# The last expert's down matrix, multiplied by column halves, and the final norm behind it

## The chip, the cores and the metric

One core of one Trainium2 chip runs the whole kernel. The metric is the device time of one launch in microseconds (us), as the median of several executions. Beside it stands one profiled execution, whose trace gives every instruction's start and duration. TensorE is called PE, VectorE DVE, ScalarE ACT, GpSimd POOL and SyncE SP, as in the profile.

## The reference, cut to what matters

A decoder block on 256 tokens of width 1024: a Mamba-2 mixer and a sparse attention mixer, merged, and then a mixture of experts over 32 experts with the top 4 per token, all in float32. The change is in the end of the expert stage and in the final norm:

```python
out = jnp.zeros_like(t)
for e in range(N_EXPERTS):
    a = clamped_swiglu(t @ w_gate_up[e] + b_gate_up[e])
    out = out + combine[:, e:e + 1] * (a @ w_down[e] + b_down[e])
...
x = x + out
return rms_norm(x, final_norm_w)      # x / sqrt(mean(x*x) + eps) * w
```

## The kernel before, in words

**Experts.** Each expert gets up to 64 of its tokens (CAP = 64). A gate/up matrix has 8 MB and a down matrix 4 MB; SP streams them through four places in SBUF of 4 MB each. PE counts finished pieces in `unit_done`, and SP waits for that count before it loads over a place. A hardware loop does most experts; the last ones are written out with finer pieces. Experts go in pairs (s = 0, 1); the last expert has s = 1.

**A down product.** With 64 tokens the stationary operand is 128 rows by 64 columns, so two matmuls can sit side by side on the two halves of TensorE's columns; `128*64` in a row of the profile says that. Before the change the two halves hold the two column halves of the result: tokens by columns 0 to 511 on partitions 0 to 63, tokens by columns 512 to 1023 on partitions 64 to 127, both in one PSUM bank. The contraction has 1024 rows, in 8 steps r of 128; partition p of the place holds rows 8p to 8p+7 of the matrix, so step r is a column range of the place. `ATL` holds the last expert's activations, transposed.

**The last down matrix.** SP loads it in five transfers by steps (`LAST_ROWS`: steps 0-1, 2-3, 4-5, 6, 7; L663 to L669). The first two wait for unit 11, the other three for unit 12, which are the two halves of the down product that used the place before. PE (L1442 to L1452) takes the steps in order, waiting for each transfer, and after step 1 runs `combine` for the expert before.

**Combine.** ACT copies the PSUM bank to SBUF (`down_out`, L1717), and `combine` (L1343 to L1353) multiplies it by the matrix of routing weights (`CTS`, 64 slots by 128 tokens) into four banks, for two token halves t and two column halves h. As h = 1 lies on partitions 64 to 127, the four matmuls have 64 rows each (`64*128`), and two sit on the two row halves of the array. `CTS` holds the weights twice, on both halves of the partitions.

**The end.** DVE adds each of the four results to X (`final_added`, L2316). ACT squares and sums each (L1768). Then each token half has its own mean, root and reciprocal. DVE multiplies token half 0 by reciprocal and norm weight (L2331, two instructions); POOL has meanwhile multiplied token half 1 by the norm weight (L834) into `XW`, which DVE and ACT scale (L2349, L1775). SP stores token half 0 in one transfer (L671), token half 1 in two (L674). A table of ACT's functions is loaded at L1764, before the squares.

Of the kernel before, what the change touches and what calls it, by code (L numbers as in the profile page):

```python
# [29 lines left out]
ALU = mybir.AluOpType  # L30
ACT = mybir.ActivationFunctionType
AX = mybir.AxisListType

P = 128
# [31 lines left out]
LAST_ROWS = ((0, 2), (2, 4), (4, 6), (6, 7), (7, 8))  # L66
# [125 lines left out]
def hybrid_block(nc, x, mix_norm_w, w_in, conv_w, conv_b, dt_bias, a_log, d_skip, ssm_norm_w,  # L192
# [3 lines left out]
    with ExitStack() as ctx:  # L196
# [149 lines left out]
        YSL2 = part(ZS, 512, 512)  # L346
# [23 lines left out]
        XW = part(ring, T * D, D)  # L370
# [9 lines left out]
        last_full = [sem(f"last_full{i}") for i in range(len(LAST_ROWS))]  # L380
# [122 lines left out]
        def _(sp):  # L503
# [161 lines left out]
            for (r0, r1), full in zip(LAST_ROWS, last_full):  # L665
                if r0 % 4 == 0:
                    sp.wait_ge(unit_done, units_to(last * 2, 11 + r0 // 4))
                sp.dma_start(places[LOOP_SLOT[9]][:, D * r0:D * r1], down_rows(EXPERTS - 1)[:, D * r0:D * r1]
                             ).then_inc(full, 16)  # L669
            sp.wait_ge(norm_ready, 2)  # L670
            sp.dma_start(out[0, 0:P], RJ[:, 0]).then_inc(stored, 16)  # L671
            for h, (normed, n) in enumerate(((norm_ready, 3), (norm_in, 1))):
                sp.wait_ge(normed, n)
                sp.dma_start(out[0, P:2 * P, 512 * h:512 * h + 512], RJ[:, 1, 512 * h:512 * h + 512]).then_inc(stored, 16)  # L674
            sp.wait_ge(stored, 16 * (T + 1))
# [3 lines left out]
        def _(pool):  # L679
# [150 lines left out]
            pool.wait_ge(wfn_ready, 2)  # L830
            for h in range(2):
                pool.wait_ge(final_in, 3 + h)
                cols = slice(512 * h, 512 * h + 512)
                g.tensor_tensor(XW[:, cols], X[:, 1, cols], WFN[:, cols], ALU.mult).then_inc(xw_ready, 1)  # L834


        @block.tensor
        def _(pe):
# [504 lines left out]
            def combine(n, s, y=YSB, first=True, final=True, halves=False):  # L1343

                pe.wait_ge(y_ready, n + 1)
                if first:
                    pe.wait_ge(o_read, n * 2 + 1)
                for t in range(T):
                    for h in range(2):
                        r = slice(64 * h, 64 * h + 64)  # L1350
                        ins = mm(psum[:, 3 + 2 * t + h, :], CTS[r, s, t], y[r, :], start=first, stop=final)  # L1351
                        if final and (h or halves):
                            ins.then_inc(o_full, 1)  # L1353
# [89 lines left out]
            for (r0, r1), full in zip(LAST_ROWS, last_full):  # L1443
                pe.wait_ge(full, 16)
                w = places[LOOP_SLOT[9]]
                for r in range(r0, r1):
                    for h in range(2):
                        ins = mm(psum[64 * h:64 * h + 64, 0, :], ATL[:, r % 4, 64 * (r // 4):64 * (r // 4) + 64],
                                 w[:, D * r + 512 * h:D * r + 512 * h + 512], start=(r == 0), stop=(r == 7))
                if r1 % 4 == 0:  # L1450
                    ins.then_inc(unit_done, 1)
                if r1 == 2:  # L1452
                    combine(last * 4 + 3, 0, final=False)
            combine(last * 4 + 4, 1, YSL2, first=False, halves=True)


        @block.scalar
        def _(act):
# [303 lines left out]
            down_out(units_to(last * 2 + 1, 8), 0, YSL2)  # L1762

            a(junk[:, 0:1], ss[:, 6:7], ACT.Sqrt)  # L1764
            for t in range(T):
                for h in range(2):
                    act.wait_ge(final_in, 2 * t + h + 1)
                    a(SQX[:, t, 512 * h:512 * h + 512], X[:, t, 512 * h:512 * h + 512], ACT.Square,  # L1768
# [606 lines left out]
```

## Time and profile before

| | us |
|---|---|
| median of 3 executions | 1250.89 |
| lowest and highest | 1250.57, 1251.33 |
| the profiled execution | 1252.41 |
| its span, first to last instruction | 1250.7 |
| PE busy in the span | 1187.8 |
| DVE, ACT, POOL busy | 438.1, 288.5, 112.6 |

The profiled execution takes 1.7 us beside its span. Times in the rows below count from the start of the span. A matmul in float32 shows as two records in the trace: `x8` in a row of L1448 or L1351 is four matmuls. The busy times are sums over the whole span and say nothing of which engine the last microseconds wait for.

### The profile page before, as it was taken

The numbers are of one execution on the slowest core, as the hardware profiler recorded it, in microseconds if no ns is written. First come the engines' busy times: TensorE is split into PE (matmuls) and PEld (weight loads), VectorE is DVE, ScalarE is ACT, GpSimd is POOL, SyncE is SP. The second block draws the span as 40 slices with busy tenths as digits, with TensorE's granted clock in tenths as the row PEclk, the third lists the DMA queues.
The fourth block names the chain that finished last, engine by engine and source line by source line (L and its number), as shares of the span: only waits on it lengthen the run. The fifth ranks groups of instructions, "written<-read, shape, count | busy, mean of one in ns | idle before, by whom it ended". The sixth has DMA issues, their size and how long they took to land.

```text
span 1250.7 us, 16280 instructions
## 1 busy us (share of the span) xinstructions
PE 1187.8 (95%) x6644; PEld 622.4 (50%) x6644; DVE 438.1 (35%) x868; ACT 288.5 (23%) x522; POOL 112.6 (9%) x99
## 2 busy tenths in 40 slices
PE   8999999999999999999999989898999989898996
PEld 8999988788743434434343424242333324242432
DVE  7876567767331221312122221212221212122112
ACT  6574457653410101101010100010110101010112
POOL 2202213345400000000000000000000000000000
PEclk9999999999999999999999999999999999999999
DMA  8747534239999999999999999999999999999995
GB/s 272 209 146 231 164 107 135 102 104 393 402 397 418 428 430 431 431 432 430 433 431 434 430 433 431 434 431 432 431 434 432 431 431 434 432 431 431 425 426 220
DMA packets 60988, 453.57 MB, mean 363 GB/s; under 512 B 9096, under 2 KB 33808, under 8 KB 45328
## 3 DMA queue, kind: packets, MB, share of 16 engines
q1 hardware_dynamic: 60640, 452.75, 88.1%
q8 instruction: 32, 0.52, 0.2%
q10 hardware_dynamic: 304, 0.20, 0.1%
q14 instruction: 12, 0.10, 0.0%
HBM read 451.88 MB, written 1.05 MB: 362 GB/s over the span
## 4 chain that ended last, share of the span: by engine, by line
PE 63%; DMA 28%; ACT 3%; DVE 3%; issue 1%; POOL 0%; SPq 0%; DVEq 0%; ACTq 0%
PE psum L1313 23%; DMA ring<-in_w_gate_up_dram 14%; DMA slot<-in_w_gate_up_dram 12%; PE psum L1325 11%; PE psum L940 9%; PE psum L1281 5%; PE psum L906 4%; PE psum L1351 3%; PE psum L842 3%; DMA ring<-in_w_down_dram 3%; PE psum L943 2%; ACT WH L1484 1%; ACT XDT L1663 1%; PE psum L1191 1%; DVE XDT L2144 1%
## 5 line engine op out<-in xcount | busy, mean ns | idle before, releaser
L1313 PE MATMUL psum<-ring,ZS 128*64 128x512 f32 x1512 | 345.9, 601 | 13.9 <-DMA ring<-in_w_gate_up_dram 13.5
L1313 PEld LDWEIGHTS psum<-ring,ZS 128*64 128x64 f32 x1512 | 105.8, 137 | 216.9 <-issue 196.8
L2290 DVE TENSOR_TENSOR X<-X,psum 128x1024 f32<-128x1024 f32 x62 | 72.9, 1218 | 373.7 <-PE psum L1351 373.6
L1325 PE MATMUL psum<-ring,HT 128*64 128x512 f32 x736 | 168.2, 610 | 22.7 <-DMA ring<-in_w_down_dram 22.7
L1313 PE MATMUL psum<-slot,ZS 128*64 128x512 f32 x512 | 119.8, 612 | 10.2 <-DMA slot<-in_w_gate_up_dram 10.2
L2272 DVE TENSOR_SCALAR ZS<-psum 128x512 f32<-128x512 f32 x32 | 22.1, 692 | 298.9 <-PE psum L1313 298.9
L1325 PEld LDWEIGHTS psum<-ring,HT 128*64 128x64 f32 x736 | 57.5, 140 | 126.1 <-issue 125.1
L1804 DVE TENSOR_TENSOR WL<-ring,WH 128x2048 fp32r<-128x2048 f32 (+1 forms) x42 | 96.1, 2287 | 38.6 <-ACT WH L1484 38.2
L1713 ACT ACTIVATE HT<-psum 128x512 f32<-128x512 f32 x31 | 18.5, 597 | 313.8 <-PE psum L842 313.8
L834 POOL TENSOR_TENSOR ring<-X,YV 128x512 f32<-128x512 f32 x2 | 2.9, 1489 | 909.9 <-DVE X L2316 909.9
L1484 ACT ACTIVATE WH<-ring 128x2048 fp32r<-128x2048 f32 (+1 forms) x42 | 78.8, 1877 | 10.7 <-PE psum L906 6.8
L1313 PEld LDWEIGHTS psum<-slot,ZS 128*64 128x64 f32 x512 | 35.3, 139 | 78.9 <-issue 61.1
L1717 ACT ACTIVATE HT<-psum 128x512 f32<-128x512 f32 x31 | 18.5, 597 | 209.8 <-PE psum L1325 209.8
L1351 PE MATMUL psum<-HT,QT 64*128 64x512 f32 x256 | 63.6, 615 | 0.0
L1281 PEld LDWEIGHTS psum<-QT,XC 128*128 128x128 f32 x480 | 54.7, 192 | 12.2 <-issue 12.2
L1281 PE MATMUL psum<-QT,XC 128*128 128x128 f32 x480 | 57.6, 278 | 0.0
L1325 PE MATMUL psum<-slot,HT 128*64 128x512 f32 x256 | 56.7, 595 | 0.0
L1709 ACT ACTIVATE ZS<-ZS 128x512 f32<-128x512 f32 x32 | 20.1, 629 | 114.5 <-DVE ZS L2272 114.5
L940 PE MATMUL psum<-HTH,WH 128*128 128x256 f32 x304 | 44.1, 288 | 0.0
L940 PE MATMUL psum<-HTL,WH 128*128 128x256 f32 x304 | 42.7, 283 | 0.0
L940 PE MATMUL psum<-HTH,WL 128*128 128x256 f32 x304 | 42.6, 283 | 0.0
L1351 PEld LDWEIGHTS psum<-HT,QT 64*128 64x128 f32 x256 | 22.0, 186 | 41.0 <-issue 41.0
(383 smaller groups left out, 1254.5 us busy)
## 6 DMA issues: line engine op xcount, KB each, us to landing
ring<-in_w_gate_up_dram SPq DMA_DIRECT2D x38, 4096.0 KB, 29.1
ring<-in_w_down_dram SPq DMA_DIRECT2D x18, 4096.0 KB, 30.7
slot<-in_w_gate_up_dram SPq DMA_DIRECT2D x12, 4096.0 KB, 28.6
ring<-in_w_gate_up_dram SPq DMA_DIRECT2D x18, 2048.0 KB, 13.2
ring<-in_w_in_dram SPq DMA_DIRECT2D x29, 1024.0 KB, 7.0
slot<-in_w_down_dram SPq DMA_DIRECT2D x7, 4096.0 KB, 30.8
ring<-in_w_down_dram SPq DMA_DIRECT2D x9, 2048.0 KB, 16.1
slot<-in_w_gate_up_dram SPq DMA_DIRECT2D x8, 2048.0 KB, 15.2
```

What stands on the lines that cost most here:

```text
L842: return nc.tensor.transpose(o, i, IDN[:, :])
L906: ins = mm(bank(b, 512), src[:, 4 * h + k, P * t:P * t + P], w[:, k, :], start=(h == 0 and n == 0 and k == 0), stop=(h == 1 and n == 2 and ...
L940: ins = mm(bank(b, 2, SEQ)[:, half], w[:, k, rows], src[:, k, :], start=(n == 0 and k == 0), stop=(n == 2 and k == KT - 1))
L943: ins = mm(bank(b, 2, nco)[:, half], src[:, k, rows], w[:, k, :], start=(n == 0 and k == 0), stop=(n == 2 and k == KT - 1))
L1281: ins = mm(bank(5 + k // 4, P, off=P * (k % 4)), H2[:, t, P * k:P * k + P], SPR[:, t].rearrange("p a b -> p (a b)"), start=(t == 0), stop= ...
L1313: ins = mm(psum[64 * (c % 2):64 * (c % 2) + 64, c // 2, :], XTS[:, k, s], every_other_run(row, c), start=False, stop=(k == KT - 1))
L1325: ins = mm(psum[64 * h:64 * h + 64, 2, :], lhs, w[:, at:at + 512], start=(k == 0), stop=(k == 7))
L1351: ins = mm(psum[:, 3 + 2 * t + h, :], CTS[r, s, t], y[r, :], start=first, stop=final)
L1484: a(WH[i % SPLITS][:, 0:n], slot_view(u, n), ACT.Copy).then_inc(wh_ready, 1)
L1804: v.tensor_tensor(WL[i % SPLITS][:, 0:n], slot_view(u, n), WHF[i % SPLITS][:, 0:n], ALU.subtract).then_inc(wl_ready, 1)
L2272: v.tensor_scalar(GBU.rearrange("p (q f) -> p q f", q=2), gu[:, :, :, 0], 7.0, None, ALU.min).then_inc(g_ready, 1)
L2290: v.tensor_tensor(xo, xo, psum[:, 3 + 2 * t:5 + 2 * t, :], ALU.add).then_inc(o_read, 1)
```

## The change: what it does

The last down matrix comes in six transfers. Step k now means the rows 4a+k of each partition for both contraction halves a = 0, 1: `k=0` and `k=1` whole (1 MB each), then k = 2 and 3 in columns 0 to 511 (512 KB each, one semaphore), then k = 2 and k = 3 in columns 512 to 1023 (512 KB each). All of them follow one wait, for unit 12. On PE the two halves of TensorE's columns hold the two contraction halves, and the column halves of the result lie in two banks. So partitions 0 to 63 and 64 to 127 of a bank are two partial sums of the same 64 tokens, and the matmul with `CTS` that follows has all 128 rows, which adds them. `combine` for the expert before moves behind the column half 0. ACT copies the two banks separately. In the norm, both token halves of columns 0 to 511 are weighted on DVE and scaled on ACT, those of columns 512 to 1023 are done on DVE, POOL does nothing, and the output leaves in two transfers by column halves. DVE squares and sums one of the four quarters.

The diff, without the renamed constants and tiles (`YL` is two tiles in place of `YSL2`, and `XW` has both token halves):

```diff
-            for (r0, r1), full in zip(LAST_ROWS, last_full):
-                if r0 % 4 == 0:
-                    sp.wait_ge(unit_done, units_to(last * 2, 11 + r0 // 4))
-                sp.dma_start(places[LOOP_SLOT[9]][:, D * r0:D * r1], down_rows(EXPERTS - 1)[:, D * r0:D * r1]
-                             ).then_inc(full, 16)
-            sp.wait_ge(norm_ready, 2)
-            sp.dma_start(out[0, 0:P], RJ[:, 0]).then_inc(stored, 16)
-            for h, (normed, n) in enumerate(((norm_ready, 3), (norm_in, 1))):
-                ...
+            last_place = places[LOOP_SLOT[9]].rearrange("p (a k n) -> p a k n", a=2, k=4)
+            last_rows = w_down[0, EXPERTS - 1].rearrange("(p a k) n -> p a k n", a=2, k=4)
+            def last_part(k, c0, c1, full):
+                sp.dma_start(last_place[:, :, k, c0:c1], last_rows[:, :, k, c0:c1]).then_inc(full, 16)
+            sp.wait_ge(unit_done, units_to(last * 2, 12))
+            last_part(0, 0, D, last_full[0])
+            last_part(1, 0, D, last_full[1])
+            last_part(2, 0, 512, last_full[2])
+            last_part(3, 0, 512, last_full[2])
+            last_part(2, 512, D, last_full[3])
+            last_part(3, 512, D, last_full[4])
+            outs = out[0].rearrange("(t p) n -> p t n", p=P)
+            for h, normed in ((0, norm_in), (1, norm_ready)):
+                cols = slice(512 * h, 512 * h + 512)
+                sp.wait_ge(normed, T)
+                sp.dma_start(outs[:, :, cols], RJ[:, :, cols]).then_inc(stored, 16)
...
-            pool.wait_ge(wfn_ready, 2)
-            for h in range(2):
-                pool.wait_ge(final_in, 3 + h)
-                cols = slice(512 * h, 512 * h + 512)
-                g.tensor_tensor(XW[:, cols], X[:, 1, cols], WFN[:, cols], ALU.mult).then_inc(xw_ready, 1)
...
+            def last_pair(k, h):
+                for a in range(2):
+                    at = 4096 * a + 1024 * k + 512 * h
+                    ins = mm(psum[64 * a:64 * a + 64, h, :], ATL[:, k, 64 * a:64 * a + 64], w[:, at:at + 512],
+                             start=(k == 0), stop=(k == 3))
+                if k == 3:
+                    ins.then_inc(unit_done, 1)
+            def last_combine(t, h):
+                mm(psum[:, 3 + 2 * t + h, :], CTS[:, 1, t], YL[h], start=False, stop=True).then_inc(o_full, 1)
+            for k in range(2):
+                pe.wait_ge(last_full[k], 16)
+                last_pair(k, 0)
+                last_pair(k, 1)
+            pe.wait_ge(last_full[2], 16 * 2)
+            last_pair(2, 0)
+            last_pair(3, 0)
+            combine(last * 4 + 3, 0, final=False)
+            pe.wait_ge(y_ready, last * 4 + 5)
+            last_combine(0, 0)
+            for k in range(2, 4):
+                pe.wait_ge(last_full[1 + k], 16)
+                last_pair(k, 1)
+            last_combine(1, 0)
+            pe.wait_ge(y_ready, last * 4 + 6)
+            last_combine(0, 1)
+            last_combine(1, 1)
...
             down_out(units_to(last * 2 + 1, 6))
-            down_out(units_to(last * 2 + 1, 8), 0, YSL2)
+            down_out(units_to(last * 2 + 1, 7), 0, YL[0])
             a(junk[:, 0:1], ss[:, 6:7], ACT.Sqrt)
+            down_out(units_to(last * 2 + 1, 8), 1, YL[1])
+            for n, (t, h) in enumerate(((0, 0), (1, 0), (0, 1))):
+                act.wait_ge(final_in, n + 1)
+                a(SQX[:, t, cols], X[:, t, cols], ACT.Square, accum_out=RT[:, 9, t, h:h + 1]).then_inc(ss_ready, 1)
+            act.wait_ge(ss_ready, 5)
             for t in range(T):
-                ...
+                act.wait_ge(lg_ready, 2 + t)
                 a(ss[:, 2 + t:3 + t], RT[:, 9, t, 1:2], ACT.Sqrt, scale=1.0 / D, bias=ss[:, t:t + 1]).then_inc(sq_root, 1)
+            act.wait_ge(lg_ready, 4)
+            for t in range(T):
+                act.wait_ge(xw_ready, t + 1)
+                a(RJ[:, t, 0:512], XW[:, t], ACT.Copy, scale=ss[:, 4 + t:5 + t]).then_inc(norm_in, 1)
...
+            final_added(0, 0, 0)
+            first_weighted(0)            # XW[:, t] = X[:, t, 0:512] * WFN[:, 0:512]
+            final_added(1, 1, 0)
+            final_added(2, 0, 1)
+            final_added(3, 1, 1)
+            dve.wait_ge(ss_ready, 4)
+            v.tensor_scalar(ss[:, 0:2], RT[:, 9, :, 0], 1.0 / D, EPS, ALU.mult, ALU.add).then_inc(lg_ready, 1)
+            dve.wait_ge(final_in, 4)
+            v.tensor_tensor_reduce(SQX[:, 1, 512:D], X[:, 1, 512:D], X[:, 1, 512:D], 1.0, 0.0, ALU.mult, ALU.add,
+                                   RT[:, 9, 1, 1:2]).then_inc(lg_ready, 1)
+            first_weighted(1)
+            dve.wait_ge(sq_root, 5)
+            v.reciprocal(ss[:, 4:6], ss[:, 2:4]).then_inc(lg_ready, 1)
+            dve.wait_ge(lg_ready, 4)
+            for t in range(T):
+                v.scalar_tensor_tensor(out=RJ[:, t, 512:D], in0=X[:, t, 512:D], scalar=ss[:, 4 + t:5 + t],
+                                       in1=WFN[:, 512:D], op0=ALU.mult, op1=ALU.mult).then_inc(norm_ready, 1)
```

## Rows read from the trace of the kernel before

**Rows 1.** The page's part 4: share of the span in the chain that ended last.

```profile
PE 63%; DMA 28%; ACT 3%; DVE 3%; issue 1%; POOL 0%; SPq 0%; DVEq 0%; ACTq 0%
```

**Rows 2.** The chain, its last transfer: start us, us, what.

```profile
1190.21 31.76 DMA ring<-in_w_down_dram
```

**Rows 3.** The issue of the five last loads (timeline: start us, us, engine, line).

```profile
1199.05 13.74 SPq L668 DMA_DIRECT2D ring<-in_w_down_dram  x5
```

**Rows 4.** Loads issued at 1199.05, 1199.4, 1202.5, 1202.9, 1205.4: KB, us to landing.

```profile
ring<-in_w_down_dram SPq DMA_DIRECT2D x1, 1024.0 KB, 30.4
...
ring<-in_w_down_dram SPq DMA_DIRECT2D x1, 1024.0 KB, 32.5
...
ring<-in_w_down_dram SPq DMA_DIRECT2D x1, 1024.0 KB, 31.9
...
ring<-in_w_down_dram SPq DMA_DIRECT2D x1, 512.0 KB, 32.7
...
ring<-in_w_down_dram SPq DMA_DIRECT2D x1, 512.0 KB, 31.5
```

**Rows 5.** PE, ACT's copy and table load from 1222 us on, in the timeline.

```profile
1222.11 3.65 PE L1325 MATMUL psum<-ring,HT 128*64 128x512 f32 x16 [1.33 <-DMA ring<-in_w_down_dram]
...
1229.76 1.89 PE L1448 MATMUL psum<-ring,ZS 128*64 128x512 f32 x8
...
1231.58 1.99 PE L1351 MATMUL psum<-HT,QT 64*128 64x512 f32 x8
...
1233.50 5.37 PE L1448 MATMUL psum<-ring,ZS 128*64 128x512 f32 x24
...
1238.91 0.60 ACT L1717 ACTIVATE ZS<-psum 128x512 f32<-128x512 f32 x1 [8.34 <-PE psum L1448]
1239.53 1.28 ACT L1764 ACT_TABLE_LOAD   x1
...
1239.57 1.99 PE L1351 MATMUL psum<-ZS,QT 64*128 64x512 f32 x8 [0.70 <-ACT ZS L1717]
```

**Rows 6.** ACT's two copies behind the 16 whole-array matmuls of L1281, in one loop pass.

```profile
1050.96 0.60 ACT L1704 ACTIVATE ZS<-psum 128x512 f32<-128x512 f32 x1 [0.62 <-PE psum L1281]
...
1052.74 0.60 ACT L1704 ACTIVATE ZS<-psum 128x512 f32<-128x512 f32 x1 [1.19 <-PE psum L1281]
```

**Rows 7.** Windows: us, busy PE, PEld, DVE, ACT, POOL, then PEclk, DMA share, GB/s.

```profile
280.00:290.00 10.00, 9.68 (x54) 7.61 (x54) 5.69 (x7) 2.74 (x4) 8.27 (x9) 1.00 1.08 320
1100.00:1150.00 50.00, 45.08 (x226) 17.72 (x223) 8.46 (x10) 4.84 (x8) 0.00 (x0) 1.00 1.00 432
1248.00:1249.00 1.00, 0.00 (x0) 0.00 (x0) 0.00 (x0) 0.00 (x0) 0.00 (x0) 0.50 0.97 379
```

**Rows 8.** The final norm in the timeline, DVE, ACT, POOL and the first store.

```profile
1240.72 1.88 DVE L2316 TENSOR_TENSOR X<-X,psum 128x512 f32<-128x512 f32 x3 [16.72 <-PE psum L1351]
...
1242.59 0.68 DVE L2316 TENSOR_TENSOR X<-X,psum 128x512 f32<-128x512 f32 x1
...
1242.75 2.94 POOL L834 TENSOR_TENSOR ring<-X,YV 128x512 f32<-128x512 f32 x2 [909.89 <-DVE X L2316]
...
1243.41 1.16 DVE L2331 SCALAR_TENSOR_TENSOR ring<-X,ss,YV 128x512 f32<-128x512 f32 x1
...
1244.56 1.68 DVE L2331 SCALAR_TENSOR_TENSOR ring<-X,ss,YV 128x512 f32<-128x512 f32 x1
...
1246.16 0.15 DVE L2326 RECIPROCAL ss<-ss 128x1 f32<-128x1 f32 x1
1246.27 0.35 SPq L671 DMA_DIRECT2D out_dram<-ring  x1
1246.41 0.72 ACT L1775 ACTIVATE ring<-ring,ss 128x512 f32<-128x512 f32 x1 [1.38 <-DVE ss L2326]
```

**Rows 9.** DVE by line and form: busy us, mean ns.

```profile
L1787 DVE CUSTOM_DVE_ANT_0 YV<-X 128x1024 f32<-128x1024 f32 x1 | 1.2, 1226 | 2.1 <-DMA X<-in_x_dram 2.1
...
L2144 DVE CUSTOM_DVE_ANT_0 XDT<-psum,CM 128x256 f32<-128x256 f32 x20 | 7.2, 418 | 0.0
```

More of the change, by code:

```diff
@@ L65 @@
 LAST_WHOLE = 3
-LAST_ROWS = ((0, 2), (2, 4), (4, 6), (6, 7), (7, 8))
+LAST_PARTS = 5
 OFF_Z, OFF_XBC, OFF_DT, OFF_Q = 0, 1024, 3072, 3088
@@ L345, in hybrid_block @@
         ATL = part(ZS, 0, 4, P)
-        YSL2 = part(ZS, 512, 512)
+        YL = [part(ZS, 512, 512), part(ZS, 1024, 512)]
         SGA = part(ZS, 1024, 512)
@@ L369, in hybrid_block @@
         RJ = part(ring, 0, T, D)
-        XW = part(ring, T * D, D)
+        XW = part(ring, T * D, T, 512)
         RCI = sb("RCI", [P, 1], I32)
@@ L379, in hybrid_block @@
         unit_done = sem("unit_done")
-        last_full = [sem(f"last_full{i}") for i in range(len(LAST_ROWS))]
+        last_full = [sem(f"last_full{i}") for i in range(LAST_PARTS)]
         x_in = [sem(f"x_in{t}") for t in range(T)]
@@ L1341, in weights_turned, with combine @@
                 ins.then_inc(ct_full, 1)
-            def combine(n, s, y=YSB, first=True, final=True, halves=False):
+            def combine(n, s, final=True):
                 pe.wait_ge(y_ready, n + 1)
-                if first:
-                    pe.wait_ge(o_read, n * 2 + 1)
+                pe.wait_ge(o_read, n * 2 + 1)
                 for t in range(T):
@@ L1350, in combine @@
                         r = slice(64 * h, 64 * h + 64)
-                        ins = mm(psum[:, 3 + 2 * t + h, :], CTS[r, s, t], y[r, :], start=first, stop=final)
-                        if final and (h or halves):
-                            ins.then_inc(o_full, 1)
+                        ins = mm(psum[:, 3 + 2 * t + h, :], CTS[r, s, t], YSB[r, :], start=True, stop=final)
+                    if final:
+                        ins.then_inc(o_full, 1)
             pe.wait_ge(h2n_ready, T)
@@ L1442, in _ @@
             pe.wait_ge(at_ready, last * 4 + 4)
[L1443 to L1450, printed above, removed]
-                    ins.then_inc(unit_done, 1)
-                if r1 == 2:
-                    combine(last * 4 + 3, 0, final=False)
-            combine(last * 4 + 4, 1, YSL2, first=False, halves=True)
+            w = places[LOOP_SLOT[9]]
+            def last_pair(k, h):
[4 more added lines that the diff above has]
+                if k == 3:
+                    ins.then_inc(unit_done, 1)
+            def last_combine(t, h):
[17 more added lines that the diff above has]
+            last_combine(1, 1)
         @block.scalar
@@ L2311, in _, with final_added @@
             gated(last * 4 + 4, units_to(last * 2 + 1, 4), last * (2 * per) + (per + base + 1))
-            def final_added(t, h):
-                dve.wait_ge(o_full, last * 8 + (2 * t + h + 7))
+            def final_added(n, t, h):
+                dve.wait_ge(o_full, last * 8 + (7 + n))
                 xo = X[:, t, 512 * h:512 * h + 512]
                 v.tensor_tensor(xo, xo, psum[:, 3 + 2 * t + h, :], ALU.add).then_inc(final_in, 1)
-            def first_half_mean(t):
-                dve.wait_ge(ss_ready, 3 + 2 * t)
-                v.tensor_scalar(ss[:, t:t + 1], RT[:, 9, t, 0:1], 1.0 / D, EPS, ALU.mult, ALU.add).then_inc(lg_ready, 1)
@@ L2336, in _, with first_weighted @@
[L2336 to L2349 removed]
+            def first_weighted(t):
+                dve.wait_ge(final_in, 1 + t)
+                v.tensor_tensor(XW[:, t], X[:, t, 0:512], WFN[:, 0:512], ALU.mult).then_inc(xw_ready, 1)
```

36 lines of the change are left out of this document (2 added, 34 removed).

## The prediction

> **What bounds the kernel now.** I read the chain of waits first. Of the whole span it runs 63% through PE and 28% through loads [rows 1]: the expert stage streams at 432 GB/s with the DMA engines at a share of 1.00 and PE busy 45.1 of 50 us [rows 7], so both are near full. Nothing of the change touches that stage, so only the last 50 us count. There the chain's last transfer, 31.76 us from 1190.21 [rows 2], is the first half of the down matrix before the last; PE starts on it at 1222.11 [rows 5], and from there PE works without a wait for data to its last down step. The reader is to see in the timeline [rows 5] that PE begins the last matrix at 1229.76 and runs 2 steps, a combine and 6 steps back to back. Step length: 6 steps in the row from 1233.50, less its pipeline tail, or 4 matmuls (x8) from 1229.76 to about 1231.48; 0.86 us per step.
>
> Then I set the landings [rows 3, 4] beside it: issue time plus flight gives 1229.5, 1231.9, 1234.4, 1235.6 and 1236.9 for steps 0-1, 2-3, 4-5, 6 and 7. PE asks for them at 1229.76, 1233.50, 1235.2, 1236.9 and 1237.8. So the loads lead PE by only 0.3 to 1.6 us, and the combine put after step 1 is what keeps PE busy while steps 2-3 arrive. The end is PE-bound with the loads close behind.
>
> After the last step (ends about 1238.7) come ACT's copy at 1238.91, the last combine at 1239.57, the first add of DVE at 1240.72, the last add's end at 1243.27, and the first store's issue at 1246.27 [rows 5, 8]. The span ends at 1250.7, 4.43 after that issue. In between the three stores, 1.05 MB, flow at 379 GB/s [rows 7], that is about 2.8 us without a pause: the end hangs on the first store's issue, not on the last one.
>
> **The change, part by part.** All durations are of the profiled execution (1252.41, of which 1.7 lie outside the span); a difference found in its span is added to the median, 1250.89.
>
> *Loads.* The wait for unit 12 delays the first two issues by 3.4 us (1199.05 to 1202.5). Their data flew 30 us behind a full queue, and what was issued before them lands until about 1227.1 (1229.5 less the 2.4 that 1 MB takes), so this costs nothing; it would cost only if the queue ran dry, which is 25 us away. SP now posts six transfers, with two pieces per partition in each. Before, the last five took 13.74 us to post as SP waited for room [rows 3]. It will now be later in posting, which is free as long as the queue keeps work; behind SP's posting wait only the stores, 30 us later. Pieces are 4 KB for k = 0, 1 and 2 KB for the column halves. The two 512 KB loads with 4 KB pieces landed 1.2 and 1.3 us after the load before, and the 1 MB ones with 8 KB pieces 2.4 and 2.5: no difference; I add 0.1 for k = 1. For 2 KB pieces the trace shows no load at a full queue. Bounds: the rate of the stage, 432 GB/s (no cost), and 320 GB/s of the stretch 280 to 290, with smaller pieces among them [rows 7]. Nearest are the stores, whose second half has 2 KB pieces: 379 at a share of 0.97, or 391 when full, 10% slower. Taken: 2.7 us per MB. Landings: k=0 1229.5, k=1 1232.0, column half 0 (k=2, 3) 1234.7, the rest 1236.1 and 1237.4.
>
> *PE.* k = 0: 1229.76 to 1231.48. The combine that filled the gap is gone from here, so PE waits until 1232.0 + 0.15 and works to 1233.87. It waits again for column half 0, to 1234.85, and works two pairs to 1236.57. Two waits, 0.67 and 0.98, that did not exist. Then combine of the expert before, 1.72. Then the first last_combine. This is a new form, 128 rows by 128 columns by 512, one at a time. Its price: L1281's matmuls are whole-array ones of 128 columns, and ACT's copies behind each eight start 1.78 us apart [rows 6], 0.2225 each, four times that at most for 512 columns, 0.89; the lower bound is that of a 64-row pair, 0.43 for each. The 64-row pairs gave four matmuls in 1.72 because two ran at once, so a single one is 0.86, as is a single one of L1281 without its overhead. Taken: 0.86. So the last combine costs 4 x 0.86 = 3.44 in place of 1.72, and partial sums added inside the array are paid with PE time. Its first quarter comes before the last columns, three quarters behind them.
>
> At each change between the forms, PE starts later than the matmul count says: 0.10 from 1231.48 to 1231.58, 0.20 from 1233.30 to 1233.50 [rows 5]. There are four changes now instead of the two before the final wait; I charge 0.10, 0.20, 0.15, 0.15. This is where a rule of the Trainium skill bears: "TensorEngine Tiling (Array Packing)", section "Key Properties", says that a change of tiling mode, not of tile, drains the engine. It gives no price. By the rule every one of the four costs something and the sum keeps its 0.6; without it the sum would be 0.6 smaller. The gaps speak for the rule.
>
> In order: combine 1236.67 to 1238.39, last_combine(0,0) 1238.59 to 1239.45, the pairs of k = 2, 3 in column half 1 (their data there since 1237.4) 1239.6 to 1241.3, then from 1241.45 three last_combines to 1244.0. ACT's copy of column half 0 (1236.6 to 1237.3) hides behind combine; the table load of 1.28 hides behind PE's work to 1241.3; the copy of half 1 takes 0.60 plus 0.2 of latency and hides behind last_combine(1,0). That hiding is the gain of the change: the 0.9 us between 1238.66 and 1239.57 go. Sum on PE: waits +1.65, combines +1.72, form changes +0.3, k=0 to the end otherwise equal, hidden copy -0.9: +2.8, and by the times above the last matmul ends at 1244.0 and not at 1241.3 (1239.57 + 1.72), +2.7.
>
> *Adds.* Before, DVE's four adds queued behind each other from 1240.72 to 1243.27; the last came 2.0 after PE's end. Now three are early, and the last starts 0.29 after PE's end (as 1240.72 stands to 1239.57 + 0.86) and ends at 1245.0: +1.7 here, so 1.0 comes back.
>
> *Norm.* On DVE behind the last add: the small mean 0.15; square-and-sum of one quarter, interpolated between 418 ns for 256 columns and 1226 for 1024 [rows 9] 0.69, plus 0.08 to read the sum; first_weighted(1) about 0.65; reciprocal 0.15: to 1246.7. ACT's roots hide behind first_weighted(1). ACT then scales two quarters, 0.72 each at most: 1248.15, and the first store is issued. DVE's two weighted products take 1.16 each, or 1.68 each where POOL ran beside it [rows 8]; POOL is idle now, so 1249.0 is taken (up to 1250.1). Before, the step from the last add's end to the first store was 3.0, now 3.15. POOL's 2.94 go, and were off the path except for the 0.5 by which a product beside it was longer.
>
> *Stores.* 1 MB in 2 KB pieces: 4.43 from first issue to the end as before, as the flow of 2.8 is the same within 0.1. The second store is issued at 1249.0, 0.85 later, while 1.4 us of the first flow: no gap. Even at 1250.1 its 1.4 us of flow and a base of 1.4 end at about 1252.9, 0.4 before the end's own tail, a loss of up to 0.7. End of the span: 1248.15 + 4.43 = 1252.6, +1.9. Forecast: 1250.89 + 1.9 = 1252.8 (a profiled execution of 1254.3).
>
> **The rivals.** About 0.2%, 2.5 us, is what can be told from no change; the forecast lies 0.6 short of that.
>
> *The waits go away (1251.1 to 1251.3).* If k = 1 and column half 0 were there when PE asks (1231.5 and 1233.2), 1.65 would go: +0.25. It would need the last loads to land 1.5 us earlier. For it: the five flights took between 30.4 and 32.7 us [rows 4], so a landing can move by 2. Against: nothing in the change makes the queue before these loads shorter, and the pieces get smaller. Chance 0.17.
>
> *Column-cut loads are slow (1255.0), the case on the slower side.* Mechanism: the flow at 320 GB/s [rows 7] instead of 431 from k = 0 on. k = 1 lands at 1233.7, column half 0 at 1236.9, the last at 1240.2. From 1233.87 on, each microsecond by which column half 0 is late moves the end by one: PE starts it at 1237.05 instead of 1234.85, +2.2, in all +4.1. The last load then still leads PE (1241.8). At full price it needs 4 KB pieces slow too, against which the 512 KB loads' 1.2 and 1.3 us speak. Chance 0.13. The Trainium skill's "DMA: Bandwidth & Descriptors", section "Bandwidth", asks for transfers of at least 1 MiB and gives 341 GB/s for one of 1 MB alone; by it the column halves would take 3.1 us per MB and the end come 0.4 later than forecast. The landings of the 512 KB loads at over 400 GB/s show no such price in a full queue.
>
> *Posting stalls.* SP posts 12 pieces per partition where it posted 5, and must find room for them [rows 3]. If the last transfer is posted so late that it lands after 1240.5, when PE needs it, the excess is added: up to 3, so 1253 to 1256. Against: posting keeps pace with draining, as in the stage. Chance 0.06.
>
> *PE's clock falls in the new waits.* It fell to 0.50 only in the idle stretch at the end [rows 7] and the stage with a wait of 1.33 before 1222.11 [rows 5] ran its steps at the same 0.86 before and after. At 1.2 GHz in place of 2.4 the remaining 9 us of work would double: about 1260. Chance 0.02.
>
> *Faster by more than 2.5 us.* Both waits gone (-1.65), whole-array matmuls at 0.43 each (-1.3 on the path) and a norm chain 1.5 shorter would all be needed, to under 1248.4. Chance 0.03.
>
> **How the numbers follow.** The forecast has 0.59, with an own range of 1251.6 to 1254.2 (form changes and new matmul -0.8 to +0.2, landings -0.3 to +0.7, norm and stores -0.3 to +0.7); about a third of it lies above 1253.4, 0.18. Slower by over 0.2%: 0.18 + 0.13 + 0.04 + 0.02 = 0.37. Faster by over 0.2%: 0.03. Within: 0.60. The range for 8 in 10 takes in the case of the waits gone and that of slow loads nearly whole: 1251.0 to 1255.2.
>
> **What would show it.** In the timeline after: L1448's successor with a gap of 0.6 to 0.7 before k = 1 and one near 1.0 before column half 0, both put down to the loads; four whole-array matmuls (`128*128 128x512`) of 0.86 each; no wait for ACT before the last two; DVE's adds with idle time between them; the first store at about 1248.2. Wrong would be: no waits of PE for data behind 1229.76; a whole-array matmul at under 0.6; last load landing after 1240; the first store before 1247.5 or after 1249; a different time at 1229.76, which would mean that the stage before has moved.

## The result

The changed kernel takes 1253.47 us (median of 12 runs, 1252.79 to 1255.43) against 1251.22 for the kernel before (12 runs, 1250.42 to 1252.92). The ratio is 1.0017, with a 95% interval of 1.0010 to 1.0025: slower by about 2.1 us, inside the 0.2% that counted as no change (the interval reaches past it), and clearly above zero. The profiled execution took 1253.09, its span 1251.3.

The profile after, the last matrix and the norm. First PE in the timeline (start us, us, engine, line, operation, tiles, shape), as [rows 5] for before:

```profile
1228.67 1.89 PE L1452 MATMUL psum<-ring,ZS 128*64 128x512 f32 x8
...
1231.02 1.94 PE L1452 MATMUL psum<-ring,ZS 128*64 128x512 f32 x8 [0.46 <-DMA ring<-in_w_down_dram]
...
1233.65 1.94 PE L1452 MATMUL psum<-ring,ZS 128*64 128x512 f32 x8 [0.70 <-DMA ring<-in_w_down_dram]
...
1235.52 1.99 PE L1354 MATMUL psum<-HT,QT 64*128 64x512 f32 x8
...
1237.44 1.12 PE L1459 MATMUL psum<-ZS,QT 128*128 128x512 f32 x2
...
1238.49 1.94 PE L1452 MATMUL psum<-ring,ZS 128*64 128x512 f32 x8
...
1240.36 2.84 PE L1459 MATMUL psum<-ZS,QT 128*128 128x512 f32 x6
```

The reader is to see the two new waits for loads in brackets, and that from 1235.52 on PE has no gap: nobody waits for ACT's copies any more. The last line is three whole-array matmuls; DVE's adds behind them, here in the timeline, start 0.86 apart because each has to wait for one of them, where before they followed each other at 0.62 [rows 8]:

```profile
1241.52 0.69 DVE L2342 TENSOR_TENSOR X<-X,psum 128x512 f32<-128x512 f32 x1 [1.51 <-PE psum L1459]
...
1242.38 0.69 DVE L2342 TENSOR_TENSOR X<-X,psum 128x512 f32<-128x512 f32 x1 [0.17 <-PE psum L1459]
...
1243.24 0.69 DVE L2342 TENSOR_TENSOR X<-X,psum 128x512 f32<-128x512 f32 x1 [0.17 <-PE psum L1459]
...
1243.96 0.69 DVE L2358 CUSTOM_DVE_ANT_0 XC<-X 128x512 f32<-128x512 f32 x1
...
1244.58 0.69 DVE L2347 TENSOR_TENSOR ring<-X,YV 128x512 f32<-128x512 f32 x1
...
1245.37 1.33 ACT L1800 ACTIVATE ring<-ring,ss 128x512 f32<-128x512 f32 x2 [0.38 <-DVE ss L2362]
1245.37 1.42 DVE L2365 SCALAR_TENSOR_TENSOR ring<-X,ss,YV 128x512 f32<-128x512 f32 x2
1246.73 0.93 SPq L683 DMA_DIRECT2D out_dram<-ring  x2
```

The loads issued at 1202.91, 1203.6, 1210.45 (k = 3, column half 0), 1218.4 and 1222.9, one row of the transfers for each, KB and us to landing. (The load of k = 2, column half 0, shares its semaphore with k = 3, so its own landing can't be read.)

```profile
ring<-in_w_down_dram SPq DMA_DIRECT2D x1, 1024.0 KB, 25.5
...
ring<-in_w_down_dram SPq DMA_DIRECT2D x1, 1024.0 KB, 27.4
...
ring<-in_w_down_dram SPq DMA_DIRECT2D x1, 512.0 KB, 23.2
...
ring<-in_w_down_dram SPq DMA_DIRECT2D x1, 512.0 KB, 16.5
...
ring<-in_w_down_dram SPq DMA_DIRECT2D x1, 512.0 KB, 13.3
```

They land at 1228.4, 1231.0, 1233.6, 1234.9 and 1236.2. Their flights are shorter than those of [rows 4], but that doesn't mean faster loads here, the loads were issued later into the same queue.

**How to compare two profiles here.** PE begins the last matrix at 1229.76 before and at 1228.67 after. That 1.1 arises before the last matrix, in matmuls that the change leaves as they are; in the other ten profiles PE begins it between 1227.67 and 1230.18. So all profiles are compared from the first matmul of the last matrix to the end of the span: 20.94 before, 22.63 after, +1.69. Column "from" in this table gives that stretch less 20.94; "ratio" is from the timed runs, each against runs of the kernel before on the same chip (us worked out with 1251.2). The first column has two limits. Spans are read to 0.1, so it is good to about 0.1. And where the first load is late, PE's wait for it lies ahead of the stretch and isn't counted: 0.46 in e4 and 0.65 in e6 by the brackets.

| kernel | from, us | ratio (95% interval) | us |
|---|---|---|---|
| changed | +1.69 | 1.0017 (1.0010 to 1.0025) | +2.1 |
| e1 combine first | +1.05 | 1.0007 (0.9997 to 1.0016) | +0.9 |
| e2 new norm alone | +0.88 | 1.0008 (0.9999 to 1.0017) | +1.0 |
| e3 norm on DVE | -1.35 | 0.9989 (0.9980 to 0.9998) | -1.4 |
| e4 half rows | +1.55 | 1.0013 (1.0004 to 1.0023) | +1.6 |
| e5 POOL beside | +2.79 | 1.0023 (1.0014 to 1.0032) | +2.9 |
| e6 one wait | -0.01 | 0.9998 (0.9989 to 1.0007) | -0.3 |
| e7 whole steps | +3.25 | 1.0031 (1.0019 to 1.0043) | +3.9 |
| e8 row halves side by side | +1.30 | 1.0008 (0.9999 to 1.0017) | +1.0 |
| e9 tokens first | -0.07 | 0.9998 (0.9989 to 1.0007) | -0.3 |
| e10 combine late | +1.49 | 1.0006 (0.9997 to 1.0015) | +0.8 |

The two columns agree within 0.7 everywhere. An interval is about 1 us to either side, so steps under 1 us are read from the profiles, one execution each, and the timed runs only say that nothing contradicts them.

### The profile page after: what moved, and what is told of

It reads as the page before. It is cut to its first block, busy times and chain, and to the rows that moved or that the text cites. A ratio compares the mean times of both kernels' runs of the same rounds, so it can differ in the third digit from the quotient of the medians.

```text
span 1251.3 us, 16275 instructions
## 1 busy us (share of the span) xinstructions
PE 1191.3 (95%) x6644; PEld 623.9 (50%) x6644; DVE 438.2 (35%) x869; ACT 289.0 (23%) x522; POOL 110.2 (9%) x97
## 3 DMA queue, kind: packets, MB, share of 16 engines
HBM read 451.88 MB, written 1.05 MB: 362 GB/s over the span
## 4 chain that ended last, share of the span: by engine, by line
PE 63%; DMA 28%; ACT 3%; DVE 3%; issue 1%; SPq 1%; POOL 0%; DVEq 0%; ACTq 0%
PE psum L1317 23%; DMA ring<-in_w_gate_up_dram 14%; DMA slot<-in_w_gate_up_dram 12%; PE psum L1329 11%; PE psum L944 9%; PE psum L1285 5%; PE psum L910 4%; PE psum L1354 3%; PE psum L846 3%; PE psum L947 2%; DMA ring<-in_w_down_dram 2%; ACT WH L1507 1%; ACT XDT L1686 1%; PE psum L1195 1%; SPq L670 1%
## 5 line engine op out<-in xcount | busy, mean ns | idle before, releaser
L1329 PE MATMUL psum<-ring,HT 128*64 128x512 f32 x736 | 171.6, 620 | 21.5 <-DMA ring<-in_w_down_dram 21.5
L1317 PE MATMUL psum<-slot,ZS 128*64 128x512 f32 x512 | 116.4, 597 | 7.7 <-DMA slot<-in_w_gate_up_dram 7.7
L944 PEld LDWEIGHTS psum<-HTH,WH 128*128 128x128 f32 x304 | 39.1, 191 | 0.8 <-issue 0.6
```

The lines of the kernel that those rows point to most:

```text
L944: ins = mm(bank(b, 2, SEQ)[:, half], w[:, k, rows], src[:, k, :], start=(n == 0 and k == 0), stop=(n == 2 and k == KT - 1))
L1317: ins = mm(psum[64 * (c % 2):64 * (c % 2) + 64, c // 2, :], XTS[:, k, s], every_other_run(row, c), start=False, stop=(k == KT - 1))
L1329: ins = mm(psum[64 * h:64 * h + 64, 2, :], lhs, w[:, at:at + 512], start=(k == 0), stop=(k == 7))
```

## The experiments

**e1: the combine back where it covers a load.**

```diff
             for k in range(2):
                 pe.wait_ge(last_full[k], 16)
                 last_pair(k, 0)
                 last_pair(k, 1)
+                if k == 0:
+                    combine(last * 4 + 3, 0, final=False)
...
-            combine(last * 4 + 3, 0, final=False)
```

> The changed kernel with one move: the combine of the expert before stands right after k = 0 again, not behind column half 0. Theory (PE bounds the end, and two waits for loads that the old combine used to fill are part of the loss): PE's waits before k = 1 and column half 0, 0.46 and 0.70 us in the profile of the changed kernel, go, and the time falls by 1.0 to 1.3 us, to 0.7 to 1.2 above the kernel before. Behind column half 0 there is then no 64-row combine left to cover ACT's copy, so up to 0.2 may come back as a wait for ACT. Rival 1 (late loads set the end): the last pairs wait for their loads instead, and the time stays within 0.3 of the changed kernel's. Rival 2 (norm and stores are the loss): no difference either, since only slack is moved.

The timed runs gave back 1.2, the profile 0.64. The waits for loads are gone, and the cover for ACT's copy with them, in the timeline of e1:

```profile
1232.59 3.65 PE L1452 MATMUL psum<-ring,ZS 128*64 128x512 f32 x16
...
1236.29 0.60 ACT L1741 ACTIVATE ZS<-psum 128x512 f32<-128x512 f32 x1 [6.87 <-PE psum L1452]
...
1236.94 1.12 PE L1459 MATMUL psum<-ZS,QT 128*128 128x512 f32 x2 [0.70 <-ACT ZS L1741]
```

I expected up to 0.2 of this wait; it is the whole 0.70 that the kernel before has too. From start to start the two waits for loads were 1.54 together and the wait for the copy is 0.92, which gives the 0.64 within 0.02. One combine can cover the loads or the copy, not both.

**e10: the same move in the kernel before.**

```diff
-                if r1 == 2:
+                if r1 == 6:
                     combine(last * 4 + 3, 0, final=False)
```

> The kernel before, with one number changed: the combine of the expert before comes behind steps 4-5 of the last matrix, not behind step 1, so it no longer fills the time in which steps 2-3 land. Theory (that cover is what the changed kernel gave away): PE waits 0.5 to 0.7 before steps 2-3 and 0.7 to 0.9 before steps 4-5, and the time rises by 1.1 to 1.4 us. Rival (the move is worth the 0.4 us that the profile of the changed kernel shows when it is undone, the rest being something else): the rise is under 0.6.

+1.49 in the profile, a little above the 1.1 to 1.4 expected, and +0.8 in the timed runs. The waits in the timeline of e10 stand where those of the changed kernel do:

```profile
1231.07 1.94 PE L1448 MATMUL psum<-ring,ZS 128*64 128x512 f32 x8 [0.46 <-DMA ring<-in_w_down_dram]
...
1233.54 1.94 PE L1448 MATMUL psum<-ring,ZS 128*64 128x512 f32 x8 [0.54 <-DMA ring<-in_w_down_dram]
```

From start to start they are 0.68 and 0.75. The cost of moving a combine out of the gap shows here without anything else of the change. The rival's bound of 0.6 is exceeded in the profile; the interval of the timed runs doesn't exclude it.

**e6: one wait for all last loads.**

```diff
-                if r0 % 4 == 0:
-                    sp.wait_ge(unit_done, units_to(last * 2, 11 + r0 // 4))
+                if r0 == 0:
+                    sp.wait_ge(unit_done, units_to(last * 2, 12))
```

> The kernel before, with all five of the last loads behind the wait for unit 12, as in the changed kernel; their sizes and pieces stay. Theory (the loads wait 25 us in the queue, so posting the first two 3.4 us later changes nothing): first issue at 1202.5, landings relative to the down product before the last as in the kernel before within 0.3, the time the same within 0.3 us. Rival (the later posting is part of the 2.1 us lost): landings 0.5 to 1.5 later, PE waits in the last matrix, and the time rises by 0.5 to 1.5.

No difference in either column, but the landings miss what I expected. The first load flew 26.3 us instead of 30.4 and landed at 1229.3. The first half of the matrix before had landed at 1220.5, so that is 8.8 later, where the kernel before has 7.45: 1.4 more and not within 0.3. PE waited 0.65 for this load, which the stretch from the first matmul leaves out. The changed wait isn't the cause as far as the trace shows. The delay already stands in the load ahead of it, the last piece of the matrix before: SP issued that at 1195.3, before the changed wait, and it landed 6.3 after the first half in place of 5.0. The changed kernel has the same late issue, and its first load landed 7.5 after the first half of the matrix before. With the timed ratio, whose interval ends at +0.9, this speaks for a late issue that costs nothing; e6's own profile doesn't show it.

**e7: the last two steps loaded whole.**

```diff
-            last_part(2, 0, 512, last_full[2])
-            last_part(3, 0, 512, last_full[2])
-            last_part(2, 512, D, last_full[3])
-            last_part(3, 512, D, last_full[4])
+            last_part(2, 0, D, last_full[2])
+            last_part(3, 0, D, last_full[3])
...
+            pe.wait_ge(last_full[3], 16)    # before last_pair(3, 0)
```

> The changed kernel without the column cut of the loads: k = 2 and k = 3 come whole, 1 MB each in 4 KB pieces; PE's order stays, so column half 0 waits for both. Theory (the loads set where PE stands before column half 0, and PE has slack only behind it): column half 0 starts about 2.3 us later than in the changed kernel, when all is there; the combine and all that follows shift with it, and the time rises by 2.0 to 2.5 us, to 4 to 5 above the kernel before. Rival (the column-cut pieces are what is late, being slow): the loads as a whole land 0.5 to 1 us earlier, and the rise is under 1.5.

+1.6 over the changed kernel in the profile, +1.8 timed: less than the 2.0 to 2.5 I expected, as step 2 is computed while step 3 arrives. In the timeline of e7:

```profile
1233.84 1.08 PE L1450 MATMUL psum<-ring,ZS 128*64 128x512 f32 x4 [0.58 <-DMA ring<-in_w_down_dram]
...
1236.33 1.08 PE L1450 MATMUL psum<-ring,ZS 128*64 128x512 f32 x4 [1.40 <-DMA ring<-in_w_down_dram]
```

The last data are there at 1236.3. From the landing of the first load to that of the last it takes 7.4 us in the kernel before (8 KB pieces, 4 KB for the last 1 MB), 7.6 in e7 (4 KB) and 7.8 in the changed kernel (2 KB for the last 2 MB); the other profiles with the same loads agree with these within 0.1. So the column cut costs the loads about 0.2, and in this order of the matmuls it is worth 1.6.

**e4 and e8: what the whole-array matmuls cost.** Both give the last combine's matmuls 64 rows again, so half of the last expert's contraction is left out of the sum.

```diff
-                mm(psum[:, 3 + 2 * t + h, :], CTS[:, 1, t], YL[h], start=False, stop=True)
+                at = 64 * h                   # e4
+                at = 64 * (t if h else 0)     # e8
+                r = slice(at, at + 64)
+                mm(psum[:, 3 + 2 * t + h, :], CTS[r, 1, t], YL[h][r, :], start=False, stop=True)
```

> The changed kernel, but the last combine uses 64 of the 128 rows (rows 0 to 63 for column half 0, 64 to 127 for column half 1), so half of the last expert's contraction is left out of the sum; all instructions are as many as before. Theory (a whole-array matmul costs PE 0.86 alone, two 64-row ones run side by side): (1,0) and (0,1) overlap, the three behind the pairs take 1.7 instead of 2.6, and a change of form less, 0.2, goes as well: the time falls by 0.8 to 1.1 us from the changed kernel. Rival (the form has no price, the loads set the end, or the adds behind them do): within 0.3 of the changed kernel. With the wait for ACT's copy before (0,1) the overlap may be partly lost: then 0.4 to 0.8.

> The changed kernel, with the last combine on 64 rows again (half of the last expert's contraction is left out), and this time the two matmuls of column half 1 on different row halves, with no wait between them, so that they can run side by side. Theory (a whole-array matmul takes PE 0.86 alone; two 64-row ones share that time): the last two end together, DVE's last two adds follow each other at 0.6 instead of 0.86, the last add starts about 0.6 earlier, and the time falls by 0.4 to 0.8 from the changed kernel. Rival (the form has no price): DVE's adds stay 0.86 apart, and the time is that of the changed kernel within 0.3.

e4 was badly made: of (1,0) and (0,1), on different row halves, the second waits for ACT's copy of column half 1 and starts when the first is nearly done, and (0,1) and (1,1) share a row half. So next to nothing ran side by side, and it gained 0.14 (0.5 timed), where I expected 0.4 or more. It says that 64 rows alone don't make a matmul cheaper. It also shows the price of one change of form: the combine before and (0,0) now have the same form, and from the start of the combine to the start of the next pairs PE takes 2.77 (1235.92 to 1238.69) in place of 2.97 (1235.52 to 1238.49). e8 has the same 2.77.

In e8 the last two are side by side: the row of the last three matmuls is 1.98 long, where it is 2.84 in the changed kernel and 2.75 in e4. DVE's last two adds close up. In its timeline:

```profile
1240.08 1.98 PE L1461 MATMUL psum<-ZS,QT 64*128 64x512 f32 x6
...
1241.24 0.69 DVE L2344 TENSOR_TENSOR X<-X,psum 128x512 f32<-128x512 f32 x1 [1.51 <-PE psum L1461]
...
1242.10 1.28 DVE L2344 TENSOR_TENSOR X<-X,psum 128x512 f32<-128x512 f32 x2 [0.17 <-PE psum L1461]
```

0.4 in the profile and 1.1 timed. Of the 0.4, 0.2 is the missing change of form. Of the 0.86 that PE saves on the last two matmuls, DVE's own pace of 0.6 for an add leaves 0.27 at the end of the last add, where I expected about 0.6.

**e2: the new norm alone.** The kernel before, with ACT's, DVE's and SP's part of the norm from the diff, and no product on POOL.

```diff
...
+            final_added(0, 0, 0)
+            first_weighted(0)
+            final_added(1, 0, 1)
+            final_added(2, 1, 0)
+            final_added(3, 1, 1)
...
```

> The kernel before, with the changed kernel's norm and stores alone: loads and matmuls stay as before, the quarters come in the order (0,0), (0,1), (1,0), (1,1). Theory (the loss is on PE): the norm is worth nothing by itself. DVE has a product of 0.69 between its first and second add, which now delays the last add by about 0.6; behind the last add the chain to the first store is 2.8 instead of 3.0, so the first store comes 0.4 later, and the time is 0.3 to 0.6 above the kernel before. Rival 2 (norm and stores make most of the 2.1): 1.5 to 2.1 above it. Beside this: with POOL idle each of DVE's weighted products takes 0.7 and not the 1.16 and 1.68 of the kernel before.

+0.88 in the profile, twice the middle of what I expected: the last add ends 14.17 after the first matmul (13.51 before), the step to the first store is 3.05, as DVE also waits 0.21 for ACT's third square, and the two stores by column halves take 4.6 from the first issue to the end in place of 4.4. DVE's two weighted products take 1.42 together with POOL idle, as expected. As it stands on the old matmuls the new norm is a loss.

**e5: POOL's products back, beside DVE.**

```diff
+            for h in range(2):
+                pool.wait_ge(final_in, 4)
+                g.tensor_tensor(XP[:, cols], X[:, 1, cols], WFN[:, cols], ALU.mult)   # nobody reads XP
```

> The changed kernel, with POOL's two products of 512 columns added beside DVE's last work; they start at the last add, write to a place that nobody reads, and nothing waits for them. Theory (POOL's products lengthen DVE's beside them, which is what the kernel before paid and the change took away): square-and-sum, first_weighted(1) and the two weighted products of DVE, 0.69 to 0.71 each in the changed kernel, grow to between 1.1 and 1.7 as long as POOL works, and the time rises by 1.0 to 2.0 us over the changed kernel, to 3 to 4 above the kernel before. Rival (DVE's long products in the kernel before came from their operands): their length stays at 0.7, the time within 0.3 of the changed kernel.

In the timeline of e5, against the changed kernel's 0.69, 0.69 and 1.42:

```profile
1242.98 0.69 DVE L2364 CUSTOM_DVE_ANT_0 XC<-X 128x512 f32<-128x512 f32 x1
1243.09 3.38 POOL L844 TENSOR_TENSOR ring<-X,YV 128x512 f32<-128x512 f32 x2 [910.62 <-DVE X L2348]
...
1243.60 1.74 DVE L2353 TENSOR_TENSOR ring<-X,YV 128x512 f32<-128x512 f32 x1
...
1245.45 2.23 DVE L2371 SCALAR_TENSOR_TENSOR ring<-X,ss,YV 128x512 f32<-128x512 f32 x2
...
1246.81 1.29 SPq L684 DMA_DIRECT2D out_dram<-ring  x2
```

DVE's products of two operands in SBUF more than double while POOL works; the square-and-sum does not change, against what I expected. The last section reads these rows further. The end is 1.1 later in the profile (0.8 timed), just by what the first store is late (from the first matmul 19.14, against 18.06). DVE's half is ready only 0.9 after the first store's issue, in the changed kernel 0.1 after it, and still the time from that issue to the end stays at 4.6.

**e3: the kernel before, with POOL's work given to DVE.**

```diff
-            for h in range(2):                       # POOL
-                pool.wait_ge(final_in, 3 + h)
-                g.tensor_tensor(XW[:, cols], X[:, 1, cols], WFN[:, cols], ALU.mult).then_inc(xw_ready, 1)
...
-            a(RJ[:, 1, 512:D], XW[:, 512:D], ACT.Copy, scale=ss[:, 5:6]).then_inc(norm_in, 1)
...
-            dve.wait_ge(xw_ready, 1)
-            v.tensor_scalar(RJ[:, 1, 0:512], XW[:, 0:512], ss[:, 5:6], None, ALU.mult).then_inc(norm_ready, 1)
+            normed(1, 0)                             # RJ = X * ss * WFN, as for token half 0
+            normed(1, 1)
```

> The kernel before, with POOL's two products and ACT's last scaling taken away: DVE does all four weighted products itself, token half 0 first, and the stores follow in the same three parts. Theory (POOL's products made DVE's two products beside them 1.16 and 1.68 long, where 0.7 is enough, and the end hangs on the first store's issue): token half 0 is done at about 1245.0 instead of 1246.24, the last product at 1246.5 instead of 1247.13, and the time falls by 1.0 to 1.3 us. Rival (the products are as long by themselves, POOL has nothing to do with it): four products of 1.16 or more follow each other, the first store comes at 1246.0 and the last at 1248.6, and the time is 0.5 to 1.5 above the kernel before.

The four products in the timeline of e3, which before were 1.16 and 1.68 [rows 8] for the first two:

```profile
1242.06 0.75 DVE L2323 SCALAR_TENSOR_TENSOR ring<-X,ss,YV 128x512 f32<-128x512 f32 x1
...
1242.79 0.74 DVE L2323 SCALAR_TENSOR_TENSOR ring<-X,ss,YV 128x512 f32<-128x512 f32 x1
...
1243.56 0.35 SPq L671 DMA_DIRECT2D out_dram<-ring  x1
1243.64 1.41 DVE L2323 SCALAR_TENSOR_TENSOR ring<-X,ss,YV 128x512 f32<-128x512 f32 x2
```

-1.35 in the profile, -1.4 timed, and an interval wholly below 1. It is the fastest kernel of the study: 1249.88 against 1251.6 for the kernel before beside it. One engine doing all of it is faster than three sharing it.

**e9: the new matrix part, the norm by token halves.** e1, with the norm of e3: squares on ACT in the order of the adds, all products on DVE, token half 0 stored first.

```diff
+            for t in range(T):
+                dve.wait_ge(sq_root, 4 + t)
+                v.reciprocal(ss[:, 4 + t:5 + t], ss[:, 2 + t:3 + t]).then_inc(lg_ready, 1)
+                ...
+                for h in range(2):
+                    v.scalar_tensor_tensor(out=RJ[:, t, at], in0=X[:, t, at], scalar=ss[:, 4 + t:5 + t], in1=WFN[:, at],
+                                           op0=ALU.mult, op1=ALU.mult).then_inc(norm_ready, 1)
```

> The changed kernel with the combine of the expert before back behind k = 0, and with the norm by token halves, all four weighted products on DVE, POOL idle, output in the order and parts of the kernel before. Theory (the end hangs on the first store, and by column halves it must wait for the sums of both token halves): token half 0 leaves about 0.9 us earlier than column half 0 did, the last quarter 0.7 behind it is not late, and the time is 0.6 to 1.0 below that of the same matrix part with the norm by column halves (which stood 1.0 above the kernel before), so 0 to 0.4 above the kernel before. Rival (the matrix part alone is the loss): as the kernel before with this norm stood 1.7 below, and the matrix part costs 1.2 or less, the time would be below the kernel before by 0.4 or more.

1.12 less than e1 in the profile, 1.1 timed. The first store leaves 16.5 after the first matmul, against 17.4 in e1, and from there to the end it takes 4.4 in place of 4.6; that is the 1.1, where I expected 0.6 to 1.0. The whole comes out at the time of the kernel before, which the theory had as its edge; the rival's lower value doesn't show, since the part that differs from e3 costs 1.28 and not under 1.2.

## Why the forecast was right, point by point

The forecast was 1252.8, +1.9; measured were +2.1 (interval +1.3 to +3.1). Its times can be held against the profile after when they are moved by the 1.1 by which that execution was ahead at the last matrix:

| | forecast, moved by -1.09 | measured |
|---|---|---|
| k = 1 and column half 0 land | 1230.9, 1233.6 | 1231.0, 1233.6 |
| last two loads land | 1235.0, 1236.3 | 1234.9, 1236.2 |
| PE starts k = 1, column half 0 | 1231.06, 1233.76 | 1231.02, 1233.65 |
| first whole-array matmul | 1237.5 | 1237.44 |
| column half 1 starts | 1238.5 | 1238.49 |
| last add ends | 1243.9 | 1243.93 |
| first store issued | 1247.06 | 1246.73 |
| span ends | 1251.5 | 1251.3 |

*The waits.* 1.65 forecast. The brackets say 0.46 and 0.70, but a bracket counts from the end of the last matmul's pipeline. From start to start, less 1.72 of work, it is 0.63 and 0.91, together 1.54. e1 and e10 show that it is the moved combine that opens them. The first load of the changed kernel landed as long after the matrix before as in the kernel before (7.5), so the later issue has no part.

*The whole-array matmuls.* 0.86 each, to be read in DVE's adds at 0.86 apart; the shorter row of e8 shows that two 64-row ones share that time.

*The changes of form.* (Form means how a matmul divides the array: `128*64`, `64*128` or `128*128`.) The sum on PE came out at +2.7 as forecast (14.3 from the first matmul to the end of the last, 1240.36 plus three of 0.86, against 11.5), with the four small gaps of 0.15 to 0.2 in it. e4 and e8 take one of the four away, and it was worth 0.20, as charged.

*The hidden copy.* The last copy costs PE nothing any more, and e1 shows the price when the cover is gone, 0.70.

*The norm.* A step that was mis-sized: the two weighted products of DVE, put at 1.16 each from [rows 8], take 0.75, and ACT's two scalings 1.33 together for 1.44. I had the contention with POOL in the rows but took the shorter of two lengthened values for the free one, and put what POOL cost the kernel before at 0.5, where e3 shows 1.35. That left the forecast unharmed only because the end hangs on the first store, which ACT's half releases: luck. The first store itself came 0.33 earlier than forecast: 0.11 from ACT's pair, the rest from DVE's instructions, which follow each other up to 0.1 closer than their durations say.

*The stores.* Put at 4.43 from the first issue to the end, as before. They take 4.6 in all seven profiles with two stores by column halves and 4.4 in all five with three stores by token halves, whether the second store follows the first closely or, as in e5, later. So a cost of 0.2 was put at nothing, and it made up for part of the 0.33 by which the first store was early. That two errors of opposite sign met here is luck too. What in the shape of the stores costs the 0.2 no run tells.

**Where the time is.** By profiles, in four steps whose sum is the whole: before to e3 -1.35 (POOL idle, DVE alone), e3 to e9 +1.28 (the new loads and matmuls, whole-array combine), e9 to e1 +1.12 (the norm split by column halves over two engines, and the stores with it), e1 to the changed kernel +0.64 (the combine out of the loads' gap, less the copy it covers): +1.69. The second step isn't PE's alone: the last add ends 1.07 later than in e3, and the other 0.2 arises in the norm, as token half 0 is now complete only with the third add and DVE waits 0.26 for ACT's root.

*The rivals.* Slow column-cut loads: e7 gives 0.2. Posting: the six loads were posted in 22.3 us, and the last was posted 11 us before it landed. The waits gone: they were there. The clock: the granted clock is 1.00 in every stretch from 1220 to 1243, and the steps before and after each wait took the same 0.86.

On the clock the prediction misread its rows. It says that the clock fell to 0.50 only in the idle stretch at the end; rows 7 show three stretches. In the whole trace of the kernel before it falls to 0.50, the level of 1.2 GHz, seven more times, for 3.4 us each, all in the expert stage, and each begins between 0.1 before and 0.8 after the end of a wait of PE of 1.98 to 2.10. Twelve waits of 1.86 to 2.11 in the same stage had no fall, and neither had the 1.33 before 1222.11 and the 1.40 in e7. In the timeline of before, 16 records with such a fall, which elsewhere take 3.65 [rows 5]:

```profile
914.76 5.27 PE L1313 MATMUL psum<-ring,ZS 128*64 128x512 f32 x16 [2.10 <-DMA ring<-in_w_gate_up_dram]
```

So that fall cost 1.6. An estimate from this: one in the new waits would have given about 1254.4, not 1260.

Still open: the steps of 0.6 to 1.1 rest on one profile each, beside intervals of 1 us. The timed difference between e1 and the changed kernel is 1.2 and that of the profiles 0.64; the intervals of the two are too wide to call this a contradiction. In e10 the landings stood 0.2 later against PE's first matmul than in the kernel before, though the loads are the same, so part of its 1.49 can be chance.

## What to carry to other kernels

A small independent piece of work on the bounding engine is worth most where that engine would wait; before moving it, write down the landings and ask which gap it fills now. Splitting a contraction over the array's column halves makes the sum somebody else's work: here a later matmul pays it at full array width. At the end of a kernel follow the first store, not the last, and keep a second engine off the operands' memory if the first can do the work in the same time.

## What the runs showed that was not expected

What DVE loses beside POOL depends on the operands and on who starts first. Some of the instructions one by one, the first from the timeline of before and the others from that of e5 (POOL's second product in before is 1.71 long and ends at 1245.69):

```profile
1242.75 1.27 POOL L834 TENSOR_TENSOR ring<-X,YV 128x512 f32<-128x512 f32 x1 [909.89 <-DVE X L2316]
...
1243.09 1.70 POOL L844 TENSOR_TENSOR ring<-X,YV 128x512 f32<-128x512 f32 x1 [910.62 <-DVE X L2348]
...
1244.76 1.71 POOL L844 TENSOR_TENSOR ring<-X,YV 128x512 f32<-128x512 f32 x1
...
1245.45 1.57 DVE L2371 SCALAR_TENSOR_TENSOR ring<-X,ss,YV 128x512 f32<-128x512 f32 x1
```

Compare the ends. A product of DVE that began while POOL was at one ended 0.55 after POOL's: 1244.57 after 1244.02 and 1246.24 after 1245.69 in before, 1245.34 after 1244.79 and 1247.02 after 1246.47 in e5. POOL's own ended 1.12 after the DVE instruction that had begun before it: 1245.69 after 1244.57 in before, and in e5 1246.47 after 1245.34 and 1244.79 after 1243.67, the end of the square-and-sum. These rows fit one reading: with two operands in SBUF on both sides, the one that came second stood still until the first was done. By it the 1.16 and 1.68 of the kernel before are two products of the same cost that arrived at different moments, and the square-and-sum kept its 0.69 in e5 because it began 0.11 before POOL, which paid for it (1.70 where its first product in before took 1.27). No run was made to test this reading.

An operand in PSUM is different. The add with one stayed at 0.68 beside POOL's first product [rows 8], and POOL's 1.27 is its shortest. Further up in the trace of the kernel before, DVE's `XC<-XC,psum` of L1905, also 128x512, takes 0.68 to 0.69 in all four of its executions, of which three lie beside a product of POOL.

In the kernel before, all this made POOL's help, 2.94 us of work taken over, a loss of 1.35.
